# Mixer input panels in another order: gate input z fourth, narrow panel with key and value fifth, index queries sixth

## What is computed

```python
def hybrid_mixer(n, w_in, ...):
    proj = n @ w_in                                    # 3408 columns
    aq, ak, av, az, aa, ab, bq, bk, bv, iq, ik, iw = split(proj)
    o_a = gated_deltanet(aq, ak, av, az, aa, ab, ...)
    o_b = dsa_attention(bq, bk, bv, iq, ik, iw, ...)
    gates = sigmoid(n @ w_gate + b_gate)               # 2 x 1024 columns
    y = gates[0] * (o_a @ w_branch_a) + gates[1] * (o_b @ w_branch_b)
    return y @ w_out

def gated_deltanet(q, k, v, z, a, b, ...):
    q, k, v = split(silu(causal_dwconv(concat(q, k, v))))
    q, k = l2_norm(q), l2_norm(k)
    g, beta = -exp(a_log) * softplus(a + dt_bias), sigmoid(b)
    decay = exp(gcum_i - gcum_j)
    m = where(strict, beta * (k @ k.T) * decay, 0)     # a triangular system per block
    u, w = triangular_solve(m + eye, [v * beta, k * beta * exp(gcum)])
    # then a scan over blocks: v_new = u - w @ S, output from S and q, new S
    return rms_norm(o) * silu(z)

def dsa_attention(q, k, v, iq, ik, iw, ...):
    q, k = rope(rms_norm(q)), rope(rms_norm(k))        # 4 query heads, one key head
    iq, ik = rope(iq), rope(rms_norm(ik))              # 8 index heads of 64
    score = einsum('bhqs,bqh->bqs', relu(iq @ ik.T), iw)
    keys = top_k(score, 64)                            # plus the 16 meta keys
    return softmax(q @ k[keys].T) @ v[keys]
```

## Time and profile before

| what | us |
|---|---|
| median of 3 runs (lowest, highest) | 1564.59 (1564.04, 1567.32) |
| the profiled execution's own time | 1566.66 |
| its span, first to last instruction | 1564.6 |
| PE busy in the span | 1549.3 |
| first mixer, its input panels and gate panels | about 30 to 200 in the span |
| second mixer, the same | about 470 to 634 in the span |

### The profile page before, as it was taken

How to read it: one execution, slowest core, us unless ns; L and a number is a source line. 1 busy time by engine, 2 the same in 40 slices (tenths; PEclk the granted TensorE clock), 3 DMA queues, 4 the chain that set the end, 5 groups by cost and what they waited for, 6 DMA issues and landing times.

```text
span 1564.6 us, 34669 instructions
## 1 busy us (share of the span) xinstructions
PE 1549.3 (99%) x12692; PEld 1517.0 (97%) x12692; DVE 1145.8 (73%) x1903; ACT 875.6 (56%) x1368; POOL 56.4 (4%) x48
## 2 busy tenths in 40 slices
PE   9999999999999999999999999999999999999999
PEld 8999899999999898999999999999999999999999
DVE  7779787766568697886666678888666757688864
ACT  6654656555455656565554555665545456466552
POOL 0100001000000010010000000000010000100000
PEclk9999999999999999999999999999999999999999
DMA  6754154655546551546655545465655535646563
GB/s 219 230 175 135 41 190 153 192 177 168 175 150 186 177 150 63 176 151 217 217 185 174 187 129 179 150 203 183 192 179 184 174 122 166 195 149 193 184 195 129
DMA packets 273486, 265.79 MB, mean 170 GB/s; under 512 B 19520, under 2 KB 271216, under 8 KB 273392
## 3 DMA queue, kind: packets, MB, share of 16 engines
q1 hardware_dynamic: 271552, 258.47, 52.8%
q0 software_dynamic: 1520, 5.93, 1.2%
...
## 4 chain that ended last, share of the span: by engine, by line
PE 88%; DVE 6%; ACT 3%; DMA 2%; issue 1%; DVEq 0%; ACTq 0%; POOL 0%; SPq 0%
PE lin L578 24%; PE lin L581 24%; PE lin L586 24%; PE aux L938 6%; PE lin L938 3%; PE lin L632 3%; DVE wL L565 1%; PE lin L603 1%; PE lin L667 1%; DVE nT L2571 1%; DMA rnk<-rows_k 1%; DVE nL L2576 1%; PE aux L586 1%; PE aux L581 1%; PE aux L578 0%
## 5 line engine op out<-in xcount | busy, mean ns | idle before, releaser
L556 ACT ACTIVATE wH<-stage 128x1024 fp32r<-128x1024 f32 x488 | 493.6, 1049 | 468.3 <-PE lin L581 322.2
L565 DVE TENSOR_TENSOR wL<-stage,wH 128x1024 fp32r<-128x1024 f32 x488 | 573.2, 1216 | 131.1 <-PE lin L586 67.9
L578 PE MATMUL lin<-nH,wH 128*128 128x256 f32 (+2 forms) x2256 | 558.0, 286 | 1.7 <-DVE u L2620 0.9
L581 PE MATMUL lin<-nL,wH 128*128 128x256 f32 (+2 forms) x2256 | 553.8, 284 | 0.0
L578 PEld LDWEIGHTS lin<-nH,wH 128*128 128x128 f32 x2256 | 424.8, 188 | 5.4 <-issue 3.2
L581 PEld LDWEIGHTS lin<-nL,wH 128*128 128x128 f32 x2256 | 425.9, 189 | 0.4 <-issue 0.2
L586 PE MATMUL lin<-nH,wL 128*128 128x256 f32 (+2 forms) x2256 | 295.0, 283 | 0.1
L586 PEld LDWEIGHTS lin<-nH,wL 128*128 128x128 f32 x2256 | 281.4, 188 | 0.4 <-DVE wL L565 0.3
L578 PE MATMUL lin<-aH,wH 128*128 128x256 f32 (+1 forms) x704 | 172.3, 284 | 0.0
L581 PE MATMUL lin<-aL,wH 128*128 128x256 f32 (+1 forms) x704 | 172.2, 284 | 0.0
L578 PEld LDWEIGHTS lin<-aH,wH 128*128 128x128 f32 x704 | 132.8, 189 | 0.0
...
## 6 DMA issues: line engine op xcount, KB each, us to landing
stage<-in_w_up SPq DMA_DIRECT2D x88, 512.0 KB, 4.5
stage<-in_ffn_w_up SPq DMA_DIRECT2D x88, 512.0 KB, 4.4
stage<-in_w_in SPq DMA_DIRECT2D x52, 512.0 KB, 4.8
stage<-in_w_down SPq DMA_DIRECT2D x40, 512.0 KB, 3.6
stage<-in_ffn_w_down SPq DMA_DIRECT2D x40, 512.0 KB, 3.5
stage<-in_w_gate SPq DMA_DIRECT2D x32, 512.0 KB, 4.9
stage<-in_even_w_in SPq DMA_DIRECT2D x24, 512.0 KB, 4.7
stage<-in_w_out SPq DMA_DIRECT2D x16, 512.0 KB, 4.0
```

Source lines behind the costliest of these rows:

```text
L556: nc.scalar.activation(wH[:, s, ks, 0:n], stage[:, s, ks, 0:n], ACT.Copy).then_inc(sem["whi"], 1)
L565: nc.vector.tensor_tensor(wL[:, s, ks, 0:n], stage[:, s, ks, 0:n], wH[:, s, ks, 0:n].bitcast(F32), ALU.subtract).then_inc(sem["wlo"], 1)
L578: mm = nc.tensor.matmul(banks[b][0:rows_, 0:width], wH[:, s, k, cols], xh, start=start and n == 0, stop=False)
L581: mm = nc.tensor.matmul(banks[b][0:rows_, 0:width], wH[:, s, k, cols], xl, start=False, stop=False)
```

## The change

The same products are computed on the same operands; places in the hand-written orders move, and with them some waits. In the input stage panel 3 is now z, panel 4 is the narrow half with bk and bv, panel 5 the index queries; 6 stays bq. So the index queries are swapped and turned by RoPE after the index key, late, instead of first. `tv` moves behind `gb1`. PE's products behind the panels are placed anew among the gate halves: bq's second half directly follows its first, gate(0, 0) comes ahead of the first index products, `index_products(1)` goes from between gate(0, 0) and gate(0, 1) to behind gate(0, 1), the halves gate(1, 0) to gate(3, 0) each stand a few steps later, and in the scan `state_seen(1)` comes before `scores(1)` and gate(3, 0) before `state_seen(2)`. DVE, ACT, POOL and SP follow. `tmp4` lies at another address. The lines of the diff that matter here:

```diff
-    ["ms1", "ssq", "ssk", "ta", "sik", "gc", "tv"]
-    + ["gb0", "gb1"] + ["kk0", "qk0", "kk1", "qk1"] + ["gb2", "kk2", "qk2"]
-    + [f"ix0{e}" for e in range(2)] + [f"ix1{e}" for e in range(4)]
+    ["ms1", "ssq", "ssk", "ta", "sik", "gc", "gb0", "gb1", "tv"]
+    + ["kk0", "qk0", "kk1", "qk1"] + ["gb2", "kk2", "qk2"]
+    + [f"ix0{e}" for e in range(2)] + [f"sbq{h}" for h in range(4)] + ["sbk"]
+    + ["Y_4"] + [x for b in range(3) for x in (f"kt{b}", f"vt{b}")] + ["X1_4", "X2_4"]
...
                         load(sp, m0 + i, s, whole(w_in, l, DC, i * 512 + s * PANEL))
-                for i, col in ((3, C_IQ), (4, 3 * 512)):
-                    for s in range(2):
-                        load(sp, m0 + i, s, whole(w_in, l, DC, col + s * PANEL))
-                load(sp, m0 + 5, 0, [(k0, k0 + 4, w_in[:, l * DC + k0:l * DC + k0 + 4, C_IK:IN_COLS]) for k0 in (0, 4)], IN_COLS - C_IK)
+                for s in range(2):
+                    load(sp, m0 + 3, s, whole(w_in, l, DC, 3 * 512 + s * PANEL))
+                load(sp, m0 + 4, 0, [(k0, k0 + 4, w_in[:, l * DC + k0:l * DC + k0 + 4, C_IK:IN_COLS]) for k0 in (0, 4)], IN_COLS - C_IK)
...
 
-                gate(0, 0)
+                load(sp, m0 + 6, 0, whole(w_in, l, DC, C_BQ))
                 sp.wait_ge(sem["att_unit"], at("att_unit", l, 1))
                 swapped(ik_s, ikr)
-                for b in range(2):
-                    kept_off(b)
-                gate(0, 1)
-                sp.wait_ge(sem["mt_out"], at("mt_out", l, 32))
-                for b in range(2):
-                    sp.dma_start(systems(U, b), diagonal(um[b], b)).then_inc(sem["mt_in"], 16)
+                kept_off(0)
+                load(sp, m0 + 6, 1, whole(w_in, l, DC, C_BQ + PANEL))
+                kept_off(1)
                 kept_off(2)
                 sp.wait_ge(sem["mt_out"], at("mt_out", l, 48))
-                sp.dma_start(systems(U, 2), diagonal(um[2], 2)).then_inc(sem["mt_in"], 16)
-                gate(1, 0)
-                gate(1, 1)
+                for b in range(3):
+                    sp.dma_start(systems(U, b), diagonal(um[b], b)).then_inc(sem["mt_in"], 16)
+                gate(0, 0)
+                for b in range(4):
+                    sp.wait_ge(lin_read[b], r0 + 6)
+                swapped(iq_s, rawT[:, 20:24, META:T])
+                gate(0, 1)
                 if l == 0:
                     sp.wait_ge(sem["scratch"], 4 * 16)
                 sp.wait_ge(sem["solved"], at("solved", l, 1))
+                gate(1, 0)
+                gate(1, 1)
...
-                w_in(6, 0)
+                turned("tv", bvT, 0, P, (lin_read[3], r0 + 5))
+                w_in(5, 0)
                 keys_and_queries(0)
                 keys_and_queries(1)
                 decays(2)
                 keys_and_queries(2)
-                w_in(6, 1)
+                w_in(5, 1)
+                for s in range(2):
+                    w_in(6, s)
 
+                gate(0, [0])
                 index_products(0)
-                gate(0, [0])
-                index_products(1)
...
                 joined(4)
+                gate(0, [1])
+                index_products(1)
+                below(5)
                 gate(1, [0])
-                below(5)
+                joined(5)
                 gate(1, [1])
-                joined(5)
 
                 def scores(j):
                     if j == 0:
 
-                gate(2, [0])
                 below(6)
                 new_values(0)
                 scores(0)
-                gate(2, [1])
+                gate(2, [0])
                 delta_out(0)
-                scores(1)
                 joined(6)
                 state_seen(1)
+                scores(1)
+                gate(2, [1])
+                new_values(1)
                 weights_turned(0)
-                gate(3, [0])
-                new_values(1)
                 weighted_values(0)
                 weights_turned(1)
+                delta_out(1)
                 scores(2)
-                delta_out(1)
+                gate(3, [0])
+                state_seen(2)
                 weighted_values(1)
-                state_seen(2)
                 weights_turned(2)
                 new_values(2)
...
 
-                index_relu(0)
                 for b in range(4):
                     act.wait_ge(lin_read[b], r0 + 7)
-                act.wait_ge(sem["rope"], at("rope", l, 1))
+                act.wait_ge(sem["rope"], at("rope", l, 2))
                 f(sq_att[:, 0:4, :], rawT[:, 16:20, :], Square)
                 f(sq_att[:, 4, :], bkr[:, :], Square).then_inc(sem["sq_att"], 1)
                 gate_hi(0, [0])
-                index_relu(1)
-                gate_hi(0, [1])
+                index_relu(0)
                 root_log([f"sbq{h}" for h in range(4)] + ["sbk"], rnb, 1.0 / P)
                 root("sbk", rnb[:, :, :], 0.0)
                 below(4)
...
-                split_lo(dve, m0 + 6, 1)
                 keys_and_queries(0)
+                split_lo(dve, m0 + 5, 1)
                 keys_and_queries(1)
+                decay_logs(2)
+                times_sin(0, "i", ik_s[:, :].unsqueeze(1), (sem["swapped"], at("swapped", l, 64)))
+                decays(2)
+                keys_and_queries(2)
+                added(0, ikr[:, :].unsqueeze(1), ik_s[:, :].unsqueeze(1))
                 dve.wait_ge(sem["rates_exp"], at("rates_exp", l, 1))
                 own.done(v.tensor_scalar(beta[:, :], beta[:, :], 1.0, None, ALU.add))
-                decay_logs(2)
-                decays(2)
-                keys_and_queries(2)
-                times_sin(1, "i", ik_s[:, :].unsqueeze(1), (sem["swapped"], at("swapped", l, 128)))
-                added(1, ikr[:, :].unsqueeze(1), ik_s[:, :].unsqueeze(1))
                 for b in range(3):
                     own.done(v.tensor_copy(sdec[:, b, :], eg[:, :, TB[b][0] + TB[b][1] - 1]))
+                split_lo(dve, m0 + 6, 0)
+                split_lo(dve, m0 + 6, 1)
+                dve.wait_ge(*read("qk2", l))
+                masked(4)
+                solved()
+                times_sin(1, "i", iq_s[:, :, :], (sem["swapped"], at("swapped", l, 128)))
+                added(1, rawT[:, 20:24, META:T], iq_s[:, :, :])
                 split_lo(dve, m0 + M_GATE, 0)
                 split_lo(dve, m0 + M_GATE, 1)
-                solved()
+                gate_lo(0, [0])
                 index_scores(0)
-                gate_lo(0, [0])
-                dve.wait_ge(*read("qk2", l))
-                masked(4)
-                index_scores(1)
...
                 state(0)
-                greatest(1)
                 normed(0)
-                gate_lo(2, [0])
                 inverse_ready(1)
                 inverse_ready(2)
+                gate_lo(2, [0])
                 unseen_values(1)
+                greatest(1)
                 split_lo(dve, m0 + M_GATE + 3, 0)
                 gate_lo(2, [1])
                 normed(1)
                 out_lo(0)
+                state(1)
+                greatest(2)
+                unseen_values(2)
+                gated(0)
                 gate_lo(3, [0])
-                greatest(2)
-                gated(0)
-                state(1)
                 normed(2)
                 out_lo(1)
-                unseen_values(2)
                 gated(1)
                 gated(2)
                 out_lo(2)
```

112 lines of the change are left out of this document (51 added, 61 removed).

## The result

| what | us |
|---|---|
| after, median of 4 runs (lowest, highest) | 1593.01 (1589.78, 1594.81) |
| before, median of 4 runs | 1564.78 |
| ratio, 95% interval | 1.0174 (1.0156 to 1.0193) |
| the profiled execution of after | 1594.81, its span 1592.7 |

The change costs 28 us. The sign of the prediction was right; its size (14.3) was half of what came, and 1593.0 lies outside 1564.5 to 1590.

A forecast was written before the change was run, and what follows sets the result against it. PE, busy 1549.3 of 1564.6 us, was taken as the bound. Waits removed and added came to +7.3 us in layer 0 and +7.0 in layer 1, clock loss unchanged: 1581.0 profiled, 1578.9 as median, range 1564.5 to 1590.

The forecast's parts named there:

- Term 1: PE's waits of gb2 for MT and of tv for bvT go: -2.2 us in layer 0, -2.5 in layer 1.
- Term 2: The moved split_lo pair shifts the wait to qk2, with 0.3 more due at kk1: +0.8 us, between 0 and 1.4.
- Term 3: PE waits for wL in gate(0, 0), behind DVE's sines and sum of the index queries: +1.0 us, up to 3.3.
- Term 4: ACT stands at gate(1, 0)'s load, now issued behind the solved systems, so rl is read late: +4.0 us per layer.
- Term 5: DVE is late with the scan's state S, and sd1 waits 0.7 us for kS1: +2.4 us, nothing without term 4.
- Term 6: DVE's softmax of block 2, normed(2), stands behind unseen_values(2), so PE waits: +1.3 us, nothing at the least.
- The clock: PE's loss to a lowered granted clock, 5.1 us before, was left at 5.1 because stalls go and stalls come.
- Rival (c): Terms 1 to 6 hold and the clock falls once more in each mixer, at 3.4 us each: 1585.7 us; chance 0.19.
- (a): solved() starts early enough that gate(1, 0) lands before PE has done sbq1, so terms 4 and 5 vanish: about 1557; chance 0.13.
- (b): ACT's wait at the load is short and the terms cancel: 1564.8 us; chance 0.10.

The follow-up runs named there:

- e4: The kernel before with only tv behind gb1 on PE and split_lo of the second bq half behind block 0's products on DVE; 0.9984 of before.
- e3: The kernel after with DVE's split_lo of gate(0, 0) before the index queries' sines and sum, and ACT's wH of gate(1, 0) later; 1.0097 of before.
- e10: The kernel of e3 with before's orders of PE, ACT, DVE and the banks from the scan on; 0.9991 of before.
- e1: The kernel after with the rest of gate(0, 0) (split_lo) ahead of the sines and sum of the index queries on DVE; 1.0189 of before.
- e2: The kernel after with wH of gate(1, 0) moved on ACT behind index_relu(0), the roots, below(4) and the reads of vt; 1.0148 of before.
- e5: The kernel after with ACT's read of o0 (delta_out(0)) ahead of gate(1) and the split_hi pair; 1.0184 of before.
- e15: The kernel of e3 with normed(2) ahead of unseen_values(2), gated(0) and the gate's read on DVE; 1.0062 of before.
- e13: The kernel after with the four DMAs that swap the index queries' rows issued by ACT instead of SP; 1.0161 of before.
- e16: The kernel of e4 with split_lo of the second bq half between the products of block 1 and block 2 on DVE; 0.9997 of before.

## Why the prediction came out half too small

**Term 1 (waits removed), right.** No wait for `bvT`, none of `gb2` for `MT`. e4 shows that this part is worth something where it stands alone.

**Term 2 (+0.8, bounds 0 to 1.4), too small.** Measured 1.25 at `kk1` and 0.80 at `qk2` in layer 0, 2.05 in all and the same in layer 1. The `qk2` part was 0.6 in the list; the step that failed is `kk1`, put at 0.3. `rnk` landed at 77.3 instead of 76.7, and I gave DVE's way from there to `decay_logs(1)` no handshakes; it holds two short waits for ACT.

**Term 3 (+1.0, bounds 1.0 to 3.3), too small: 3.5 and 2.5.** The sum was said to end at 106.9 and ended at 110.4. `solved()` was on time (104.5). What failed is a step that I had not written down at all: that the swap has landed and POOL's cosines are done when `solved()` ends. The swap landed at 105.7, so DVE waited 1.15 for it, and 2.30 more for POOL, which ran beside DVE's sines. The second of these waits stood in the trace of before, and I had misread it: "with DVE idle" is wrong for the earlier trace rows, since DVE's sines ran beside that product and DVE then stood 2.31 us ahead of the sum. The first two rows are before, the others after:

```profile
69.67 1.23 DVE L2145 TENSOR_TENSOR iq_s<-iq_s,c 128x1024 f32<-128x1024 f32 x1
73.20 1.23 DVE L2138 TENSOR_TENSOR rawT<-rawT,iq_s 128x1024 f32<-128x1024 f32 x1 [2.31 <-POOL rawT L914]
...
105.73 3.45 POOL L912 TENSOR_TENSOR rawT<-rawT,c 128x1024 f32<-128x1024 f32 x1 [23.65 <-DMA iq_s<-rawT]
...
105.69 1.23 DVE L2142 TENSOR_TENSOR iq_s<-iq_s,c 128x1024 f32<-128x1024 f32 x1 [1.15 <-DMA iq_s<-rawT]
109.22 1.23 DVE L2135 TENSOR_TENSOR rawT<-rawT,iq_s 128x1024 f32<-128x1024 f32 x1 [2.30 <-POOL rawT L912]
```

From the start of the sines to the end of the sum the pair takes 4.8 us in both, not the 2.4 of my list. My upper bound had the right partner, POOL against DVE, and a like size (2.3 us); I took the lower one "because `solved()` is mostly small instructions", and where the two did meet in `solved()` (layer 1 of after, e3, e10) it was one small copy of 0.38 us that stood for 1.8 to 2.4. The rule of the Trainium skill, taken at its word, would have given 3.3 here, the nearest of all my figures to 3.5. In layer 0 that is in part luck: the two met behind `solved()` and not in it, and the late swap is no part of the 3.3.

**Term 4 (+4.0 in each layer), right as a mechanism, wrong in how it adds.** ACT stood at the load and `rl` was read at 119.7 instead of the forecast 117.3: SP needed 7.3 us instead of 5.8 from `Bt` to the end of `A<-za`, and the two DMAs of the half were there only at 116.6 and 118.8. But the wait of PE stands once, 3.8 us in layer 1. In layer 0 it is hidden by term 3 and the half clock. Without term 3 (e1) it is 4.8 and 6.7 us, larger than I had it. Terms 3 and 4 were added up; they lie side by side on the way to the same place, so that the larger counts, and taking away one gives nothing (e1) or some 4 us (e2), both 12. That the load's place behind the solved systems is the cause was tested only from ACT's side (e2, e3); a kernel with the loads of gate(1, 0) and gate(1, 1) back ahead of `zx` was not run.

**Term 5 (+2.4), right place, too small: 4.2 and 4.0.** DVE's late `S` was the reason given and is a real one: e5, which takes ACT's part away, still waits 3.1 and 3.0 for it. The estimate of DVE's lateness (1.7 to 2.3) fell short by about 1, and the 0.7 that was added for `sd1` behind `kS1` did not come. What I missed is ACT: `kS1` takes the bank of `o0`, which `delta_out(0)` reads behind three passes of `gate(1)` and a `split_hi` pair, 5.4 us in all. I had walked DVE's list to that point and not ACT's. The wait of 0.7 for `PT` in each layer was missed in the same way.

**Term 6 (+1.3), right: 1.5 in both layers**, and some 5.5 us with its share of the clock (e15).

**The clock (left at 5.1), wrong.** This is the step that failed most dearly: no price for the slow clock behind new waits. "Stalls go and stalls come" treated them as alike: those that went were 0.3 to 2.2 us long, those that came 1.5 to 4.2 us, most with small products behind them. Busy time lost is 12.5 us instead of 5.1. Rival (c) had the direction but one fall per mixer; there were three. With waits of 19.8 us in place of 14.3 and 8.3 us of busy time on top, the 28 us are there. Had I dropped the two falls of before and given each of the three places of a mixer the price of a fall in the earlier trace rows, 1.7 to 3.4 us, the forecast would have been 1578.9 - 5.1 + 6 x 1.7 to 6 x 3.4, that is 1584 to 1594. It could not have been sharp: the falls differ from one execution to the next. The 23 executions of before beside e13 to e16 have a mean granted clock of 1.000 in the fastest (1560.2 us) and 0.993 in the slowest (1570.3 us), so that the 5.1 us which I read from one profile are no fixed cost of before either.

**Rivals (a) and (b)** are excluded: `Bt` was ready at 104.5, as the list had it, not by 101, and ACT's wait at the load was long. Of the signs named for the case that the prediction holds, ACT's wait at the load, the missing wait for `MT` of block 0 and the wait for `Pm` were seen in both layers. The wait for `wL` was there but two to three times as long; PE's wait for `rl` stood in layer 1 alone; and the wait ahead of `kS1` ended with ACT's `oA`, not with DVE's `S`.
